# A tuned two-block transformer kernel: the high and low parts of a weight unit made in two halves, in the midst of the running unit

## The reference

```python
h = rms_norm(x, norm_mix_pre);  q, k, v, u, gates = split(h @ w_in)            # block 1
y_a = chunk_band_attention(q, k, v, rel_bias) @ w_attn_out                     # 8 heads of 64
y_b = multiscale_pool(u, w_group, scale) @ w_pool_out
x = x + rms_norm((g_a * y_a + g_b * y_b) @ w_o)
x = x + rms_norm(conv_gated_ffn(rms_norm(x), w_up, conv_w, conv_b, w_down))    # d_ff 2816
proj = rms_norm(x) @ w_in_2                                                    # block 2, 4 heads
o_a = gated_delta_rule_chunked(conv+silu of q_a, k_a, v_a, g, beta)            # a scan over chunks
o_b = diff_attention(rope(q_b), rope(k_b), v_b, lam)                           # p0 - lam * p1
x = x + concat(norm(o_a) * silu(z_a), norm(o_b) * silu(z_b)) @ w_out_2
```

## Time and profile before

| | |
|---|---|
| median of 3 runs | 1107.69 us (1105.7 to 1107.75) |
| the profiled execution | 1107.15 us, its span in the trace 1105.7 us |
| PE, busy in the span | 1062.4 us (96%) |
| DVE / ACT / POOL | 648.6 / 434.8 / 101.3 us |
| mean granted TensorE clock | 0.986 of full |
| instructions | 15210 |

### The profile page before, as it was taken

How to read it: one execution, slowest core, us unless ns; L and a number is a source line. 1 busy time by engine, 2 the same in 40 slices (tenths; PEclk the granted TensorE clock), 3 DMA queues, 4 the chain that set the end, 5 groups by cost and what they waited for, 6 DMA issues and landing times.

```text
span 1105.7 us, 15210 instructions
## 1 busy us (share of the span) xinstructions
PE 1062.4 (96%) x6156; PEld 837.9 (76%) x6156; DVE 648.6 (59%) x1121; ACT 434.8 (39%) x767; POOL 101.3 (9%) x84
## 2 busy tenths in 40 slices
PE   7999999999999999999999999898999998988998
PEld 5777777778778888888888888667776876866776
DVE  6645454566438787777772122674576475575474
ACT  6233232344443544444443222343353353354431
POOL 1000000000210000000001000411120120120210
PEclk9999999999999999999999999998999899999899
DMA  8221313122321333332332333121111111211102
GB/s 334 83 85 58 94 59 92 61 77 76 114 95 58 96 114 98 112 96 95 95 95 79 112 114 108 61 78 57 59 53 44 58 40 48 68 39 40 39 20 76
DMA packets 25429, 90.72 MB, mean 82 GB/s; under 512 B 2880, under 2 KB 3136, under 8 KB 25232
## 3 DMA queue, kind: packets, MB, share of 16 engines
q1 hardware_dynamic: 23328, 83.90, 24.0%
q0 software_dynamic: 592, 3.54, 0.8%
q10 hardware_dynamic: 1440, 2.31, 0.6%
HBM read 87.64 MB, written 2.10 MB: 81 GB/s over the span
## 4 chain that ended last, share of the span: by engine, by line
PE 81%; DVE 11%; ACT 5%; issue 2%; DMA 1%; POOL 0%; SPq 0%; ACTq 0%; DVEq 0%; POOLq 0%
PE PS L521 22%; PE PS L524 21%; PE PS L522 21%; PE PS L555 3%; DVE Wl L1032 2%; DVE C L1580 2%; PE PS L770 1%; ACT Wh L1700 1%; PE PS L637 1%; PE PS L1005 1%; PE PS L1002 1%; PE PS L1003 1%; PE PS L650 1%; PE PS L660 1%; DVE Hl L1046 1%
## 5 line engine op out<-in xcount | busy, mean ns | idle before, releaser
L521 PE MATMUL PS<-Hh,Wh 128*128 128x512 f32 x848 | 349.8, 412 | 0.6 <-ACT M L1820 0.6
L522 PE MATMUL PS<-Hl,Wh 128*128 128x512 f32 x848 | 333.9, 394 | 0.0
L524 PE MATMUL PS<-Hh,Wl 128*128 128x512 f32 x848 | 333.9, 394 | 0.0
L1032 DVE TENSOR_TENSOR Wl<-raw,Wh 128x1024 fp32r<-128x1024 f32 x155 | 189.3, 1226 | 201.3 <-ACT Wh L1700 200.1
L521 PEld LDWEIGHTS PS<-Hh,Wh 128*128 128x128 f32 x848 | 161.0, 190 | 43.5 <-issue 11.0
L1700 ACT ACTIVATE Wh<-raw 128x1024 fp32r<-128x1024 f32 x155 | 161.5, 1051 | 77.6 <-PE PS L524 65.4
L524 PEld LDWEIGHTS PS<-Hh,Wl 128*128 128x128 f32 x848 | 161.0, 190 | 35.4
L522 PEld LDWEIGHTS PS<-Hl,Wh 128*128 128x128 f32 x848 | 161.4, 190 | 30.3 <-issue 1.4
L521 PE MATMUL PS<-Ah,Wh 128*128 128x512 f32 x176 | 69.8, 396 | 0.0
L522 PE MATMUL PS<-Al,Wh 128*128 128x512 f32 x176 | 69.8, 396 | 0.0
L524 PE MATMUL PS<-Ah,Wl 128*128 128x512 f32 x176 | 69.8, 396 | 0.0
(11 more groups left out here) (310 smaller groups left out, 1484.1 us busy)
## 6 DMA issues: line engine op xcount, KB each, us to landing
raw<-in_w_units SPq DMA_DIRECT2D x155, 512.0 KB, 3.5
relb<-in_rel POOLq DMA_DIRECT2D x1, 2048.0 KB, 9.7
out<-X ACTq DMA_DIRECT2D x8, 256.0 KB, 2.1
X<-in_x SPq DMA_DIRECT2D x3, 512.0 KB, 7.2
X<-in_x SPq DMA_DIRECT2D x2, 256.0 KB, 4.4
raw<-in_w_units SPq DMA_DIRECT2D x2, 256.0 KB, 4.7
rope<-in_rope POOLq DMA_DIRECT2D x1, 512.0 KB, 4.1
mats<-in_mats POOLq DMA_DIRECT2D x1, 384.0 KB, 3.5
```

Of the source, the lines that this page charges most:

```text
L521: pe.matmul(bank, Wh[:, s, w], rhs[0](r), start=first and j == 0, stop=False)
L522: pe.matmul(bank, Wh[:, s, w], rhs[1](r), start=False, stop=False)
L524: ins = pe.matmul(bank, Wl[:, s, w], rhs[0](r), start=False, stop=last and end)
L1032: dv.tensor_tensor(Wl[:, s, :], raw[:, s, :], Wh[:, s, :].bitcast(F32), sub).then_inc(unit_split, 1)
```

## The change

The whole-unit instructions stay where a unit is not run by `unit`. Inside `unit` they are cut in two: ScalarE makes the first 512 columns of `Wh` of unit n + 2 at step 2 and the other 512 at step 4, VectorE the halves of `Wl` at steps 4 and 6. `unit_rounded` now counts two per unit, so that a half of `Wl` waits for its own half of `Wh`; PE and SP still wait for the whole unit (`unit_split`, told by the second half). 58 of the 156 units are made so (29 in the attention of block 1, 29 in block 2): 58 instructions `128x1024` become 116 of `128x512` on each of the two engines. PE's list stays as it was.

```diff
--- before.py
+++ after.py
@@ -52,6 +52,9 @@
 RING = 4
 
 AHEAD = 2
+
+
+HIGH_STEPS, LOW_STEPS = (2, 4), (4, 6)
 
 
 C_MIXPRE, C_MIXPOST, C_FFNPRE, C_FFNPOST, C_NORM2 = 0, 8, 16, 24, 32
@@ -292,6 +295,7 @@
 
 
     landed = [semaphore(f"unit_landed{s}") for s in range(RING)]
+
     unit_rounded, unit_split = semaphore("unit_rounded"), semaphore("unit_split")
     unit_used = semaphore("unit_used")
 
@@ -1028,14 +1032,25 @@
             if n >= N_UNITS:
                 return
             s = n % RING
-            dv.wait_ge(unit_rounded, n + 1)
+            dv.wait_ge(unit_rounded, 2 * n + 2)
             dv.tensor_tensor(Wl[:, s, :], raw[:, s, :], Wh[:, s, :].bitcast(F32),
                              sub).then_inc(unit_split, 1)
 
+        def split_half(n, h):
+
+            if n < N_UNITS:
+                s, own = n % RING, slice(h * HALF, (h + 1) * HALF)
+                dv.wait_ge(unit_rounded, 2 * n + h + 1)
+                ins = dv.tensor_tensor(Wl[:, s, own], raw[:, s, own], Wh[:, s, own].bitcast(F32), sub)
+                if h:
+                    ins.then_inc(unit_split, 1)
+
         def unit(n, read):
 
-            split(n + AHEAD)
-            yield from idle(KT)
+            for m in range(KT):
+                if m in LOW_STEPS:
+                    split_half(n + AHEAD, LOW_STEPS.index(m))
+                yield
             dv.wait_ge(unit_used, n + 1)
             read()
             yield
@@ -1137,7 +1152,7 @@
                         dv.tensor_tensor(Wl[:, 0, 0:HALF], raw[:, 0, 0:HALF],
                                          Wh[:, 0, 0:HALF].bitcast(F32), sub).then_inc(half_split, 1)
                     if k == 1:
-                        dv.wait_ge(unit_rounded, 1)
+                        dv.wait_ge(unit_rounded, 2)
                         dv.tensor_tensor(Wl[:, 0, HALF:], raw[:, 0, HALF:],
                                          Wh[:, 0, HALF:].bitcast(F32), sub).then_inc(unit_split, 1)
                     if k in (3, 5):
@@ -1697,11 +1712,22 @@
             ac.wait_ge(landed[s], 16 * (n // RING + 1))
             if n >= RING:
                 ac.wait_ge(unit_used, n - RING + 1)
-            ac.activation(Wh[:, s, :], raw[:, s, :], ACT.Copy).then_inc(unit_rounded, 1)
+            ac.activation(Wh[:, s, :], raw[:, s, :], ACT.Copy).then_inc(unit_rounded, 2)
+
+        def round_half(n, h):
+
+            if n < N_UNITS:
+                s, own = n % RING, slice(h * HALF, (h + 1) * HALF)
+                ac.wait_ge(landed[s], 16 * (n // RING + 1))
+                if n >= RING:
+                    ac.wait_ge(unit_used, n - RING + 1)
+                ac.activation(Wh[:, s, own], raw[:, s, own], ACT.Copy).then_inc(unit_rounded, 1)
 
         def unit(n, behind=None):
-            round_unit(n + AHEAD)
-            yield from idle(KT)
+            for m in range(KT):
+                if m in HIGH_STEPS:
+                    round_half(n + AHEAD, HIGH_STEPS.index(m))
+                yield
             if behind:
                 behind()
             yield
@@ -1738,7 +1764,7 @@
                     if k == 1:
                         ac.wait_ge(landed[0], 16)
                         ac.activation(Wh[:, 0, HALF:], raw[:, 0, HALF:],
-                                      ACT.Copy).then_inc(unit_rounded, 1)
+                                      ACT.Copy).then_inc(unit_rounded, 2)
                     if k in (3, 5):
                         round_unit(k // 2)
                 for k in range(KT):
```

## The result

Median 1092.22 us (1090.82 to 1093.05, 4 runs) against 1106.7 us for the kernel before beside it (1105.3 to 1107.75, 4 runs); ratio 0.9875, 95% interval 0.9859 to 0.9891. The profiled execution took 1093.05 us, its span is 1091.6 us. The forecast was 1092.

The account below looks back on a forecast made before the run. PE was taken as the bound, its waits mostly ended by DVE. Gains of 1.6 + 2.9 + 8.2 + 1.85 = 14.6 us, plus 2.1 for clock, less 1.7 for new waits, gave 15.0 off 1107.15: 1092 us, range 1085 to 1103.

Parts of the forecast that it names:

- Attention, 1.6: Block 1's attention, pairs 1 to 3: PE's wait of 0.55 us goes in each, 1.6 us in all.
- Stage 0, 2.9: Block 2, stage 0: PE's waits of 0.69 us (`head_LmT`) and 2.22 us (ScalarE's copy) both go whole; lower bound 1.7.
- Stages 1 and 2, `head_VN`, `head_Vb`, level two: Block 2, per stage: 1.4 of 1.57 us goes at `head_VN`, all 1.05 at `head_Vb`, all 2.10 at the second level.
- `head_Oa`, 0.45: Stages 1 and 2: a half of `Wl` now ahead of `head_Oa` costs 0 to 0.68 us per stage, taken as 0.45.
- Stage 3, 1.85: Block 2, stage 3: 1.4 us gained at `head_VN`, 1.1 at one `head_Wd`, 0.65 lost at the next; net 1.85.
- What is late next, 1.7: Block 2: links with small slack become new PE waits, between 0 and about 6 us, taken as 1.7 us lost.
- Cut overhead at nothing: All 58 units: halves add 8.1 us busy time on DVE and 12.1 on ACT, hidden in idle time, so no cost.
- Clock, 2.1: Block 2: clock falls follow about every other long PE wait; removing those waits gives half of 4.3 us, 2.1.
- Rival 1: The next wait takes half of the gain, as links that PE feeds can't come earlier: 1100 us, chance 0.20.
- Rival 2: DVE's queue isn't freed, its head waiting for `Wh` as long at the new place: 1107 us, chance 0.07.
- rival 3: Slower: halves in 24 rows of scores, in attention and stages 1 to 3, delay PE uncovered: 1114 us, chance 0.06.
- Rival 4: With the waits, all 31.8 us at the lower clock go too, up to 15.9 us more: 1077 us, chance 0.05.

Follow-up runs that it names:

- experiment 5: Against the changed kernel, ScalarE as before (whole `Wh` at step 0), VectorE's halves of `Wl` still at steps 4 and 6: 1094.21 us.
- 3: Cut but not moved: against the kernel before, both halves of `Wh` and of `Wl` at step 0, where the whole units stood: 1105.23 us.
- 4: Moved but not cut: against the kernel before, the whole `Wh` at step 2 and the whole `Wl` at step 4: 1089.17 us.
- experiment 6: Changed kernel with POOL's first product of the keys' rotation done for 16 of 512 columns: 1087.97 us.
- experiment 12: Changed kernel with the two key products `L1466` and `L1467` in stage 3 done for one of four tiles: 1093.45 us, 2 runs.
- 9: The changed kernel run once more, unchanged, to see whether the clock's falls belong to the kernel: 1092.21 us.
- 10: The kernel with whole, uncut units at steps 2 and 4 run once more, beside the changed kernel: 1090.58 us.
- the moved kernel: Kernel with the whole `Wh` at step 2 and whole `Wl` at step 4, not cut: 1089.17 us, and 1090.58 us when run once more.

## Why the prediction was right, and where it was right by luck

1092 against 1092.2. The mechanism stands: VectorE's list was what PE waited for (experiment 5), and the place of the split in it, not its size, is what counts (3 and 4). But the size is the sum of errors that nearly cancel: at one clock the gain is 10.4 us where I had 14.6 - 1.7 = 12.9, and the clock gave 3.5 where I had 2.1.

- **Attention, 1.6.** Mis-sized: a pair is 1.22 us shorter and not 0.55, since the matmuls behind the wait had held some of it, 3.7 in all. The step left out is the first pair, where two halves ahead of `pool_in` cost 1.0 us; its wait of 0.79 us was in the trace of before:

```profile
33.87 0.65 PE L624 MATMUL PS<-ident,pool_sum 128*128 128x128 f32 x4 [0.79 <-DVE pool_in L1071]
```

  Net 2.7 at one clock.
- **Stage 0, 2.9.** Failed. "I take both whole" was wrong for ScalarE's copy: 2.22 fell to 1.29, by 0.93, near the 1.04 of the `Wh` that had stood ahead. `Yc` did not come earlier against PE: ScalarE's row that reads it began 1.19 us after PE's L779 before and 1.18 us after the same matmuls now. The lower bound, 1.7, was right. Two waits of 0.55 and 0.72 us took its place.
- **Stages 1 and 2, `head_VN`, `head_Vb`, level two.** Right: 1.29 of 1.57 where I had 1.4, all of 1.05, all of 2.10.
- **`head_Oa`, 0.45.** The worst step. It cost 1.54 and 1.52 us, twice the upper bound of 0.68, because that bound came from a half with no POOL beside it; without the keys' product it is 0.45 (experiment 6), which was a choice between 0 and 0.68 and met the number by luck. POOL's two-operand product had its row at that very place in the trace of before, and the mask product beside POOL was already slow there; I looked for the half's duration and not for its neighbour. VectorE, then POOL, before:

```profile
807.94 1.35 DVE L1370 TENSOR_TENSOR head_DT<-head_DT,mats 128x512 f32<-128x512 f32 x1
```

```profile
808.70 1.75 POOL L2209 TENSOR_TENSOR heads_Kr<-heads_Kr,rope 128x512 f32<-128x512 f32 x1
```

  So a stage lost 2.9 us of idle PE and not 4.1.
- **Stage 3, 1.85.** Failed: idle PE is 8.6 us where it was 8.3. `head_VN` gave 1.3 and the last `head_Wd` grew by 0.61, both as said. The other `head_Wd` kept 1.23 of 1.31: the whole `Wl` there stood beside a chain from PE that is as long: VectorE now waits 0.73 us for PE's L769 in its place, and POOL's product then holds a row of four columns (experiment 12). `heads_Kr` (0.80) and a `head_VN` (0.65) are new.
- **What is late next, 1.7.** About right: the new waits of stages 0 and 3 make 2.7, less 0.41 for the one for `sq` that went.
- **Cut overhead at nothing.** Borne out to within a microsecond: uncut is 0.7 us faster at one clock, and the raw times don't separate.
- **Clock, 2.1.** 3.5 measured. The reason I gave, a fall for every other long wait, fits the count in experiments 9 and 10 (9 of 15), and the four waits of 2.10 us and more with their falls are gone. My reading of the first was short: the clock fell at 762.4, during the wait, and stayed low for 6.8 us, not 5.3. But most falls stand at no long wait, and some differ between executions of one kernel with the same waits; what brings those is open. So the term is right in kind, and its size is as much the mean over executions (0.9856 and 0.9902) as these waits.

Rival 1 (the next wait takes half) came true in stages 0 and 3 and nowhere else. Rival 2 and rival 3 did not occur: VectorE's waits for the halves' `Wh` are 9.0 us in all, and in stages 1 and 2 no row of scores waits. Two signs came out otherwise than I had written: four of these waits in block 2 are over 1 us (2.49, 1.94 and twice 1.31), and PE has six waits over 0.9 us in the four stages and not two. Rival 4 came true by some 3.5 of its 15.9 us. "PE idles some 8 us" in block 2 was wrong, it is 13.7.

## What to carry to other kernels

An instruction that is urgent for nobody should stand behind the urgent ones of its engine's list, at a step where its operand has been ready for a while; where it stands is worth more than how finely it is cut. Before putting one at a new place, look at what the other engines do there, and take its duration from a row with the same company. And where two versions are 2 us apart, compare them at one granted clock, or over many executions, before explaining the difference. Where a VectorE product with both operands in SBUF meets one of POOL, take POOL's end plus the time that VectorE's columns need behind it (0.54 us for 512 here), not the duration of either alone.

## Not expected of the hardware

- A VectorE product with both operands in SBUF takes 1.77 us beside POOL's product and 0.70 where POOL does 16 columns (128x512), 2.31 against 1.23 (128x1024); with an operand in PSUM it takes 0.68 beside POOL too. It ends 0.53 to 0.55 us (512 columns) or 1.09 us (1024) after POOL's. A `TENSOR_SCALAR` of four columns out of SBUF ended with POOL's instruction, 0.74 us against 0.15.
- A profiled execution stood at 1.2 GHz for 12 to 38 us of some 1090, and 3.4 us of this cost 1.6 to 1.75 us in a stage; of the changed kernel's seven low stretches five came at the same places in a second execution. A low stretch ahead of a wait of PE can hide the wait: 1.27 us in one profile of the moved kernel, none in the other.
